# Rounding and splitting three plain units of an FFN input group as whole slots of four blocks

## What the reference computes

```
h = x
h = h + 0.5 * swiglu_ffn(h, ffn_norm[0, 0], ffn_w_in[0, 0], ffn_w_out[0, 0])
h = h + mlstm_mixer(rmsnorm(h, mix_norm[0]), ...)
h = h + 0.5 * swiglu_ffn(h, ffn_norm[0, 1], ffn_w_in[0, 1], ffn_w_out[0, 1])
return rmsnorm(h, final_norm)

def swiglu_ffn(x, g, w_in, w_out):
    a, b = jnp.split(rmsnorm(x, g) @ w_in, 2, axis=-1)
    return (jax.nn.silu(a) * b) @ w_out
```

## Time and profile before

| | |
|---|---|
| median of 3 runs | 1832.39 us (1832.05 to 1832.68) |
| the profiled execution's own time | 1832.95 us |
| its span, first to last instruction | 1831.0 us |
| TensorE, VectorE, ScalarE busy | 99%, 72%, 51% of the span |
| mean granted TensorE clock | 0.999 of full speed |
| one FFN input group, from start to start | 42.45 us |

### The profile page before, as it was taken

One profiled execution on the slowest core, in us unless ns is written; L12 is line 12 of the kernel. 1 busy time (PEld: TensorE's weight loads), 2 busy tenths in 40 slices (PEclk: granted clock), 3 DMA queues, 4 the chain that ended last, 5 costly groups with the idle time before them and its releaser, 6 DMA issues.

```text
span 1831.0 us, 21540 instructions
## 1 busy us (share of the span) xinstructions
PE 1814.1 (99%) x8164; PEld 1499.2 (82%) x8164; DVE 1316.8 (72%) x1490; ACT 941.0 (51%) x1050; POOL 38.4 (2%) x53
## 2 busy tenths in 40 slices
PE   8999999999999999999999999999999999999998
PEld 6888888888888888888888888888888888888886
DVE  6888888888755554655478757888888888754444
ACT  6555555555654444444445545555555555653442
POOL 0000000000100000000000000000000000000000
PEclk9999999999999999999999999999999999999999
DMA  7666665566566566566655556666665566556663
GB/s 226 218 210 206 199 206 184 185 205 202 173 191 192 189 190 188 162 184 200 191 149 156 168 183 184 225 211 204 193 203 184 190 202 206 195 185 200 194 191 138
DMA packets 180607, 350.67 MB, mean 192 GB/s; under 512 B 10848, under 2 KB 11040, under 8 KB 180256
## 3 DMA queue, kind: packets, MB, share of 16 engines
q1 hardware_dynamic: 179952, 348.17, 59.9%
q0 software_dynamic: 432, 1.18, 0.3%
q10 hardware_dynamic: 128, 0.03, 0.0%
HBM read 347.24 MB, written 2.10 MB: 191 GB/s over the span
## 4 chain that ended last, share of the span: by engine, by line
PE 98%; DVE 1%; ACT 1%; issue 0%; DMA 0%; DVEq 0%; ACTq 0%
PE acc L428 49%; PE acc L492 8%; PE acc L490 8%; PE acc L491 8%; PE aux L490 7%; PE aux L492 7%; PE aux L491 7%; PE aux L485 1%; PE aux L457 1%; PE aux L702 1%; PE aux L690 0%; DMA h<-in_x_dram 0%; ACT sums L788 0%; PE aux L652 0%; ACT u_hi L766 0%
## 5 line engine op out<-in xcount | busy, mean ns | idle before, releaser
L1150 DVE TENSOR_TENSOR w_lo<-raw,w_hi 128x1024 fp32r<-128x1024 f32 x336 | 410.9, 1229 | 327.9 <-ACT w_hi L751 325.8
L751 ACT ACTIVATE w_hi<-raw 128x1024 fp32r<-128x1024 f32 x336 | 354.4, 1059 | 347.6 <-PE acc L428 336.9
L428 PE MATMUL acc<-w_hi,g_hi 128*128 128x512 f32 x704 | 274.9, 390 | 0.0
L428 PE MATMUL acc<-w_hi,g_lo 128*128 128x512 f32 x704 | 274.0, 389 | 0.0
L428 PE MATMUL acc<-w_lo,g_hi 128*128 128x512 f32 x704 | 273.9, 389 | 0.0
L428 PE MATMUL acc<-w_hi,u_hi 128*128 128x512 f32 x512 | 205.2, 401 | 2.8 <-DVE w_lo L1150 2.8
L428 PE MATMUL acc<-w_hi,u_lo 128*128 128x512 f32 x512 | 200.6, 392 | 0.0
L428 PE MATMUL acc<-w_lo,u_hi 128*128 128x512 f32 x512 | 200.3, 391 | 0.0
L1232 DVE TENSOR_TENSOR w_lo<-raw,w_hi 128x1024 fp32r<-128x1024 f32 x112 | 135.2, 1223 | 51.1 <-ACT w_hi L826 51.1
L826 ACT ACTIVATE w_hi<-raw 128x1024 fp32r<-128x1024 f32 x112 | 116.4, 1057 | 87.5 <-PE aux L492 46.4
L428 PEld LDWEIGHTS acc<-w_hi,g_lo 128*128 128x128 f32 x704 | 132.2, 188 | 27.7
(11 more groups left out here) (228 smaller groups left out, 3208.1 us busy)
## 6 DMA issues: line engine op xcount, KB each, us to landing
raw<-in_ffn_w_in_dram SPq DMA_DIRECT2D x248, 512.0 KB, 4.6
raw<-in_ffn_w_out_dram SPq DMA_DIRECT2D x176, 512.0 KB, 4.7
raw_more<-in_ffn_w_in_dram SPq DMA_DIRECT2D x104, 512.0 KB, 4.6
raw<-in_a_w_in_dram SPq DMA_DIRECT2D x96, 512.0 KB, 4.3
raw<-in_a_w_out_dram SPq DMA_DIRECT2D x32, 512.0 KB, 4.4
h<-in_x_dram SPq DMA_DIRECT2D x4, 512.0 KB, 8.9
final_gain<-in_final_norm_dram POOLq DMA_DIRECT2D x1, 1024.0 KB, 5.2
out_dram<-h SPq DMA_DIRECT2D x1, 1024.0 KB, 3.9
```

Source lines behind the costliest of these rows:

```text
L428: mm = nc.tensor.matmul(acc[:, TT * (c % 2) + t, :], s[:, k, tok], w[:, ring, kk, :], start=(k == 0 and n == 0), stop=(k == GK * granules ...
L751: nc.scalar.activation(w_hi[:, n % RING], raw[:, n % RING], ACT.Copy)\
L1150: nc.vector.tensor_tensor(w_lo[:, n % RING], raw[:, n % RING], w_hi[:, n % RING].bitcast(F32), ALU.subtract)\
```

## The change

Units 2, 4 and 6 of every group are rounded by one activation of all four blocks (128x2048) in place of two of 128x1024, and split by one subtraction of 128x2048 in place of two. Both count their semaphore up by two at their end. `high_whole` waits for both loads of the unit and for the second half of item n-3; `low_whole` waits for the full count of `pair_high`. Units 0 and 7 stay in halves. TensorE's, SP's and GpSimd's lists are the same as before.

```
+            def high_whole(i, group, u):
+
+                n, unit = item(group, u), len(UNITS) * group + u
+                act.wait_ge(left_landed[unit % SLOTS], landings(i, unit))
+                act.wait_ge(right_landed[unit % SLOTS], landings(i, unit))
+                free(i, n, 1)
+                nc.scalar.activation(hi_slots[n % SLOTS], raw_slots[unit % SLOTS], ACT.Copy)\
+                    .then_inc(pair_high, 2)
...
                     high_mixed(i, group, 1, 1)
-                    high_plain(i, group, 2, 0)
-                    high_plain(i, group, 2, 1)
+                    high_whole(i, group, 2)
                     high_straight(i, group, 3)
...
-                    high_plain(i, group, 6, 0)
-                    high_plain(i, group, 6, 1)
+                    high_whole(i, group, 6)
                     keep_first(i, group)
...
+            def low_whole(i, group, u):
+
+                n, unit = item(group, u), len(UNITS) * group + u
+                dve.wait_ge(pair_high, halves(i, n) + 2)
+                nc.vector.tensor_tensor(lo_slots[n % SLOTS], raw_slots[unit % SLOTS],
+                                        hi_slots[n % SLOTS].bitcast(F32), ALU.subtract).then_inc(pair_low, 2)
...
-                    low_plain(i, group, 6, 0)
-                    low_plain(i, group, 6, 1)
+                    low_whole(i, group, 6)
                     low_plain(i, group, 7, 0)
                     low_plain(i, group, 7, 1)
```

More of the change, by code:

```diff
@@ L896, in ffn_in @@
                     high_mixed(i, group, 3, 1)
-                    high_plain(i, group, 4, 0)
-                    high_plain(i, group, 4, 1)
+                    high_whole(i, group, 4)
                     keep_hidden(i, group, 1)
@@ L1384, in ffn_in @@
                         low_mixed(i, group, 1, 1)
-                    low_plain(i, group, 2, 0)
-                    low_plain(i, group, 2, 1)
+                    low_whole(i, group, 2)
                     mix_weights(i, group, 3)
@@ L1390, in ffn_in @@
                     low_mixed(i, group, 3, 1)
-                    low_plain(i, group, 4, 0)
-                    low_plain(i, group, 4, 1)
+                    low_whole(i, group, 4)
                     mix_weights(i, group, 5)
```

## The result

The changed kernel takes 1845.72 us (median of 6 runs, 1845.44 to 1846.57), the kernel before 1832.41 beside it (6 runs, 1831.94 to 1833.32): a ratio of 1.0072, 95% interval 1.0061 to 1.0082, 13.3 us slower. 1843.6 was forecast. The profiled execution has a span of 1843.5 us and a time of its own of 1845.59, 12.6 above the profiled one of before.

A forecast was written before the change was run, and what follows sets the result against it. TensorE, busy 99% of the span, was taken as the bound; 18 transitions between groups at 0.62 us of late drains gave 11.2 us, added to the median 1832.39 for 1843.6 us, range 1836.5 to 1849.

The forecast's parts named there:

- hidden after all: Rival: VectorE makes up 0.41 us more between unit 6 and the straight split, so no change; 1832 to 1836, chance 10%.
- A transition: Passage from one FFN group to the next, 18 in all; late drains were to cost TensorE 0.62 us at each.
- 0.11 comes back: At TensorE behind a stall, the second weight load follows after 0.11 us where the pace is 0.23, regaining about 0.11.
- ends at 258.40, and VectorE starts at 258.43: At unit 6, the whole activation's end on ScalarE and the whole split's start on VectorE, 0.03 us apart.
- On the edge, and worth nothing by itself: Unit 6's split would be there at 260.77 against TensorE's first weight load at 260.76, so no loss there.
- TensorE waits for anything three times over in the whole listing: Reading of TensorE's waits before the change: 3.9, 2.8 and 1.3 us, none in an FFN input group.
- The weighed rule: Skill's advice on larger or broken-up instructions; first half would make the change a gain, second a loss; prediction sided with the second.
- The load: Second load for unit 1, issued later, lands at 265.9 against the mixing's need at 266.50: hidden with 0.6 us to spare.
- The clock: Rival: new pauses bring TensorE down to 1.2 GHz for the 24 matmuls that follow, 99 us, 1932; chance 1%.
- More comes late: Rival: unit 1's load lands too late, or whole pairs take 0.5 us more, delaying units 2 and 4; 1852.5, chance 9%.

The follow-up runs named there:

- the first four experiments: Changed kernel with whole slots only at unit 6 (1846.36 us), only at units 2 and 4 (1832.80), only on ScalarE (1846.12), only on VectorE (1833.09).

## Why the prediction was right

**The place and the mechanism.** Right in its path: unit 6 is the one that counts (all of the loss with it alone, none with units 2 and 4), what makes it late is ScalarE's activation, which waits for the second half of unit 4 with all its work still to do (all of the loss with it alone, none with the long subtraction alone), and TensorE pays at `drain_left` and `drain_last`, 18 times each (half of the loss is left when `drain_right` and `drain_last` are moved forward, none that the medians show when `drain_left` is too). The rival "hidden after all" would have needed 0.41 us more room; the kernel that is whole on VectorE used up 0.49 and had none left.

**The lengths.** The whole activation was put at 1.92 and took 1.92 us, the whole split 2.29 and took 2.29. `keep_first` was put 1.85 behind the activation's start (258.33) and started 1.83 behind.

**The terms that were too small.** A transition was put at 0.62 us and measured 0.73, so the loss was put at 11.2 us where 13.3 were measured, and the forecast was 2.1 us low. The 0.11 can be followed in the trace. In the prediction's terms the load behind `drain_last` comes 0.73 late, and 0.11 comes back. The last load before unit 6 stood here in the kernel before:

```profile
260.53 0.19 PEld L492 LDWEIGHTS acc<-w_hi,u_lo 128*128 128x128 f32 x1
```

From it to the load behind `drain_last` it was 274.36 - 260.53 = 13.83 us; in the changed kernel it is 277.51 - 262.86 = 14.65, so that load is 0.82 late, 0.09 more than expected. Of this 0.07 is the step "ends at 258.40, and VectorE starts at 258.43": I took the 0.03 us between ScalarE's end and VectorE's start from the row with a split of 128x1024. A whole split starts 0.10 behind (260.75 to 260.85), and so did the straight split of 128x1536 already in the earlier trace rows (266.70 + 1.49 = 268.19, start at 268.30), which was the nearer row. The other 0.02 is the start of the whole activation, 2.35 us behind that of the row before (256.48 to 258.83) where TensorE was 2.33 behind (260.53 to 262.86). Behind `drain_last` 0.12 came back, and the slower loads after the stall cost 0.03, a term that the prediction did not have: 0.82 - 0.12 + 0.03 = 0.73. With two more subtractions in the kernel before, where no slot is whole, the transition also read 0.62 in place of 0.57, and there too the loads behind the stall were slower for a while. What slows them stays open.

**Unit 6 itself.** "On the edge, and worth nothing by itself" held in the main. Its first load was late by 0.1 us, of which all but 0.01 came back at once, and the slower loads behind it lost another 0.02 to 0.04. With the drains late this adds nothing to the transition, as the prediction said, since the load behind `drain_last` comes when VectorE is done; with all drains moved forward it is what is left, 0.02 to 0.04 us a group.

**A view that was too narrow.** The prediction's "TensorE waits for anything three times over in the whole listing" is read from the waits of matmuls. The view of the weight loads' waits names one that this view lacks, 0.3 us at `drain_last` in a single group, so the place that became the limit had already been one once. It changes the sum by little, but it was a sign of how thin the cover was there.

**The weighed rule.** The Trainium skill, Perfetto Trace Analysis, "Optimizing Scalar/DVE Operations", says that larger operations can improve throughput if the engine is saturated, and that where ScalarE or VectorE isn't saturated but causes bubbles on others, breaking instructions up may let work be completed sooner. VectorE was freed of 12.3 us of recorded busy time (1316.8 to 1304.5) and the kernel became 13.3 us slower. So it is the second part that bears on this kernel, read the other way round: instructions that had been broken up were joined, and bubbles came. The experiments narrow it down to one of them, ScalarE's at unit 6.

**The rivals.** The load was no matter: the mixing follows without idle time at 268.93. The clock stayed at 1.00, the level of 2.4 GHz, in the window of a group with two stalls, so that rival fell. "More comes late" would have needed a late load or a late unit 2 or 4, and the view of the weight loads' waits names neither a split of these units nor a load of weights.

## What to carry to other kernels

Joining two instructions that wait for two halves of the same buffer joins the waits too: the first half's work can no longer be done ahead, and the engine behind gets both at the end. Price such a change by the idle stretches between that place and the next thing that the bounding engine waits for, not by the engine's idle time in total (5.4 us a group here, of which only the 0.56 ahead of unit 7 and the 0.40 behind the mixing of unit 1 lay on that way). What waits last need not be what was changed: here the changed unit arrived 0.1 us late and TensorE made nearly all of that good, while the drains behind it, the last of which had had 0.06 us to spare, cost the time, and moving the three drain calls forward hid all but 0.02 to 0.04 us a group again.

## What the runs showed of the hardware

VectorE's start behind an activation that it waited for went with the size of VectorE's own instruction, not with ScalarE's: 0.03 us for a split of 128x1024 behind an activation of 128x1024 or of 128x2048, 0.10 for a split of 128x2048 behind either, and the same within rounding for 128x1536 behind 128x1536 (0.11 by the rows above). It was so wherever VectorE was idle ahead of such a split, in the traces of the kernel before, the changed kernel and the first four experiments. Why is not shown.

A short wait of TensorE at a weight load is mostly given back, but not for nothing. The second load follows after 0.11 to 0.12 us in place of 0.23 where the wait was 0.1 us or more, and the ten or so loads behind it come slower, by up to 0.07 us together: 0.04 behind the 0.1 us at unit 6 in the timeline above. The kernel with one more subtraction, 0.61 us more work with 0.49 absorbed, lost up to 0.03 us a group.
